# Modulation sums of a two-block transformer kernel: one-hot columns in four column groups, rows turned on VectorE

## What is computed

```python
# block one, layer l: six vectors of 1024
c_act = jax.nn.silu(c)
mod = c_act @ w_ada[l] + b_ada[l]
sh1, sc1, g1, sh2, sc2, g2 = jnp.split(mod, N_MOD, axis=-1)
h = modulate(rms_norm(x, mixer_norm_g[l]), sh1, sc1)
...
x = x + g1[:, None, :] * (mixed @ w_out[l])
h2 = modulate(rms_norm(x, ffn_norm_g[l]), sh2, sc2)
...
# block two, layer l: nine vectors of 1024
mod = (c_act @ ada_w[l] + ada_b[l])[:, None, :]
h = rmsnorm(x, norm_pre[l, 0]) * (1.0 + sc1) + sh1
y = swiglu(h, ffn_w_gate[l, 0], ffn_w_up[l, 0], ffn_w_down[l, 0])
x = x + 0.5 * g1 * rmsnorm(y, norm_post[l, 0])
```

## Time and profile before

| | |
|---|---|
| median of 3 runs (lowest to highest) | 2015.21 us (2014.39 to 2019.77) |
| profiled execution: its own time, its span | 2018.86 us, 2017.0 us |
| PE, PEld busy | 1937.6 us (96%), 1547.6 us (77%) |
| DVE, ACT, POOL busy | 1289.5 us (64%), 735.5 us (36%), 70.3 us (3%) |
| chain of waits, by engine | PE 70%, DVE 18%, issue 4%, ACT 4%, SP 2%, DMA 1%, POOL 1% |
| `ada_sum` on PE (L726) | 444 records, 52.1 us busy |
| moved by DMA | 546.99 MB, mean 271 GB/s |
| mean granted TensorE clock | 0.976 of full speed |

### The profile page before, as it was taken

How to read it: one execution, slowest core, us unless ns; L and a number is a source line. 1 busy time by engine, 2 the same in 40 slices (tenths; PEclk the granted TensorE clock), 3 DMA queues, 4 the chain that set the end, 5 groups by cost and what they waited for, 6 DMA issues and landing times.

```text
span 2017.0 us, 29866 instructions
## 1 busy us (share of the span) xinstructions
PE 1937.6 (96%) x11691; PEld 1547.6 (77%) x11691; DVE 1289.5 (64%) x2018; ACT 735.5 (36%) x1248; POOL 70.3 (3%) x111
## 2 busy tenths in 40 slices
PE   7999899998999899998999999999999999999998
PEld 7888645555888645545999887899989998878887
DVE  5999423435998324335788757666668887575555
ACT  2021222223021222224433556544464436555445
POOL 0101000000201000000000002000000000110000
PEclk6999799999999799999999999999999999999999
DMA  9859899997858799998599842677638996526651
GB/s 352 306 167 326 320 414 406 406 419 272 290 177 314 312 408 402 418 413 300 209 328 349 272 126 84 231 247 254 216 126 292 327 349 158 147 75 205 202 189 40
DMA packets 266958, 546.99 MB, mean 271 GB/s; under 512 B 31042, under 2 KB 187212, under 8 KB 242252
## 3 DMA queue, kind: packets, MB, share of 16 engines
q1 hardware_dynamic: 266828, 545.19, 74.7%
HBM read 544.08 MB, written 4.22 MB: 272 GB/s over the span
## 4 chain that ended last, share of the span: by engine, by line
PE 70%; DVE 18%; issue 4%; ACT 4%; SPq 2%; DMA 1%; POOL 1%; DVEq 0%; ACTq 0%; POOLq 0%
PE ps L859 11%; PE ps L783 10%; PE ps L709 8%; DVE acc L2083 6%; PE ps L960 6%; PE ps L740 4%; PE ps L742 4%; PE ps L741 4%; PE ps L811 3%; PE ps L770 3%; DVE arena L2217 3%; DVE wsp L2138 2%; PE ps L772 2%; PE ps L926 2%; SPq L444 2%
## 5 line engine op out<-in xcount | busy, mean ns | idle before, releaser
L2138 DVE TENSOR_TENSOR wsp<-ring,wsp 128x1024 fp32r<-128x1024 f32 x264 | 321.5, 1223 | 173.6 <-ACT wsp L1625 166.8
L1625 ACT ACTIVATE wsp<-ring 128x1024 fp32r<-128x1024 f32 x264 | 277.9, 1056 | 322.7 <-PE ps L742 196.1
L740 PE MATMUL ps<-hsp,wsp 128*128 128x256 f32 x1120 | 319.6, 285 | 5.0 <-DVE hsp L2613 3.0
L741 PE MATMUL ps<-hsp,wsp 128*128 128x256 f32 x1120 | 316.9, 283 | 0.0
L742 PE MATMUL ps<-hsp,wsp 128*128 128x256 f32 x1120 | 316.8, 283 | 0.0
L709 PE MATMUL ps<-arena,ring 128*128 128x256 f32 x1280 | 283.0, 381 | 4.1 <-PE ps L709 2.7
L709 PEld LDWEIGHTS ps<-arena,ring 128*128 128x128 f32 x1280 | 242.8, 191 | 39.0 <-issue 5.0
L783 PE MATMUL ps<-wsp,asp 128*128 128x512 f32 x1056 | 255.4, 394 | 1.6 <-DVE wsp L2138 0.2
L859 PE MATMUL ps<-ring,hpick 128*64 128x512 f32 x1024 | 230.5, 603 | 8.1 <-issue 8.1
L783 PEld LDWEIGHTS ps<-wsp,asp 128*128 128x128 f32 x1056 | 194.1, 188 | 50.1 <-DVE wsp L2138 9.7
L740 PEld LDWEIGHTS ps<-hsp,wsp 128*128 128x128 f32 x1120 | 214.8, 192 | 7.7 <-DVE wsp L2138 3.6
(11 more groups left out here) (280 smaller groups left out, 2778.3 us busy)
## 6 DMA issues: line engine op xcount, KB each, us to landing
ring<-in_w_expert_gate_dram SPq DMA_DIRECT2D x64, 1024.0 KB, 8.8
ring<-in_w_expert_up_dram SPq DMA_DIRECT2D x64, 1024.0 KB, 11.1
ring<-in_w_expert_down_dram SPq DMA_DIRECT2D x64, 1024.0 KB, 10.3
ring<-in_ada_w_dram SPq DMA_DIRECT2D x48, 1152.0 KB, 9.3
ring<-in_ffn_w_gate_dram SPq DMA_DIRECT2D x44, 1024.0 KB, 11.8
ring<-in_ffn_w_up_dram SPq DMA_DIRECT2D x44, 1024.0 KB, 13.9
ring<-in_ffn_w_down_dram SPq DMA_DIRECT2D x44, 1024.0 KB, 5.2
ring<-in_w_ada_dram SPq DMA_DIRECT2D x32, 1152.0 KB, 12.0
```

The lines of the kernel that those rows point to most:

```text
L740: mm(dst, hi, v_hi, start=start, stop=False, skip_group_check=True)
L741: mm(dst, hi, v_lo, start=False, stop=False, skip_group_check=True)
L1625: act_(split_part(at % SPLITS, 0, n), piece(unit, n), ACT.Identity).then_inc(S.whi, 1)
L2138: v_.tensor_tensor(split_part(at % SPLITS, 1, n), piece(unit, n), split_part(at % SPLITS, 0, n, F32), ALU.subtract).then_inc(S.wlo, 1)
```

## The change

- `ada_sum` gives way to `row_sum` for all units but unit 11 of block two. The stationary operand is now a window of 32 columns of `onehot` in which one column is ones and the others zeros; the moving operand is `acc`. `acc` is cut into four sets of six strips of 32 columns, and each set goes to a column group of the array of its own (PSUM partitions 0 to 31, 32 to 63, 64 to 95, 96 to 127) with 192 moving columns. So there are four matmuls of 128 x 32 by 128 x 192 where there were six of 128 x 128 by 128 x 1. The column that holds the ones chooses the row in which the unit's sums land; the other rows receive zeros, and all units of a stage add up in one bank, one row each.
- DVE adds no bias per unit. `turn_sums` transposes the bank once per stage in blocks of 32 x 32 (128 x 192) into `rowcols`, waits for it, and `add_rows` adds the bias for all units at once. The five adds of a mixer become one, and so do the eight of block two's f = 0; PE no longer waits for DVE to read a bank.
- In the opening the 32-column window of unit `u` in `chot` holds `c_act` instead of ones; blocks that PE takes from the ring go the same way. Of unit 2 PE takes blocks 4 to 7, DVE 0 to 3 (`OPENING = (6, 6, 4)`).
- `four` of f = 0 is written out twice on PE and DVE, since the window is a constant of the instruction. ACT and SP keep their loop.

```diff
-MODS = 11
+MODS = 4
+HOT, ROWS = 8, 32
+OPENING = (6, 6, 4)
...
+            def row_of(bank, v, window, start):
+
+                v = v.rearrange("p (k j n) -> p j k n", k=AC, j=P // ROWS)
+                for j in range(P // ROWS):
+                    last = mm(ps[j * ROWS:(j + 1) * ROWS, bank, 0:AC * ROWS], window, v[:, j], start=start, stop=True,
+                              skip_group_check=True)
+                return last
+
+            def row_sum(n, slot, bank, row, start):
+
+                pe.wait_ge(S.ada_acc, n + 1)
+                row_of(bank, acc[:, slot, :], hot(onehot, row), start).then_inc(S.ada_sum, 1)
...
-                def ada_later(u, bank, read):
-
-                    pe.wait_ge(S.ada_mod, read)
-                    ada_sum(u - AHEAD, (u - AHEAD) % 2, bank)
+                def ada_later(u):
+
+                    row_sum(u - AHEAD, (u - AHEAD) % 2, 4, u - AHEAD, start=(u == AHEAD))
...
                             if f == 0:
 
-                                pe.wait_ge(S.ada_mod, i * 4 + j + units_in(2) + MODS * l)
-                                ada_sum(i * 4 + j + 12 * l, j % 2, 3)
+                                row_sum(i * 4 + j + 12 * l, j % 2, 3, i * 4 + j, start=(i == 0 and j == 0))
...
-                    if f:
-                        four(0)
-                        four(1)
-                    else:
-                        with pe.Fori(0, 2) as i:
-                            four(i)
+                    four(0)
+                    four(1)
...
+            def turn_sums(ready, count, bank):
+
+                eng.wait_ge(ready, count)
+                own.link(v_.transpose(rowcols[:], ps[:, bank, 0:AC * ROWS]))
+
+            def add_rows(u, n, bias_at):
+
+                def units(v, at):
+                    return v[:, at:at + n * AC].rearrange("p (u k) -> p u k", u=n)
+                v_.tensor_tensor(units(mod, u * AC), summed(0, n), units(vA, u * AC + bias_at), ALU.add
+                                 ).then_inc(S.ada_mod, 1)
...
                 conv(1)
-                mod1(3, 5)
-                mod1(4, 4)
                 conv(2)
...
-                mod1(5, 5)
-                mod1(6, 4)
                 ada1(7)
...
+                turn_sums(S.ada_sum, 8 - AHEAD, 4)
+                add_rows(AHEAD, 8 - AHEAD, ROWS_1["ada"][0])
+                eng.wait_ge(S.ada_mod, 2)
                 ahead1(0)
-                mod1(7, 4)
                 ahead1(1)
...
-                            if f == 0:
-                                mod2(i * 4 + AHEAD + j)
...
                     if f == 0:
+                        turn_sums(S.ada_sum, 8 + 12 * l, 3)
+                        add_rows(AHEAD, 8, 0)
+                        eng.wait_ge(S.ada_mod, 2 + MODS * l)
```

More of the change, by code:

```diff
@@ L391, in release, with hot, summed @@
                 eng.sem_inc(free[unit % RING][part], 1)
-        def units_in(u):
-            return u - 1 if u >= AHEAD else 1
+        def hot(v, row):
+            return v[..., HOT - row:HOT - row + ROWS]
+        def summed(row, n=1):
+            return rowcols[:].rearrange("p (k u) -> p u k", k=AC)[:, row:row + n, :]
         def clear(eng, sems, go):
@@ L1119, in _ @@
             S = opening
-            pe.wait_ge(init_v, 1)
+            pe.wait_ge(chot_w, 1)
             for u in range(AHEAD):
[L1122 to L1127, removed]
-                last.then_inc(free[u % RING][1], 1)
[L1129 to L1134, removed]
+                for k in range(OPENING[u], KD):
+                    if k == OPENING[u] and k < 6:
+                        wait_landed(pe, 0, 0, u, parts=(0,))
+                    elif k == 6:
+                        wait_landed(pe, 0, 0, u, parts=(1,))
+                    last = row_of(6, wada(u)[:, k, :], hot(chot[:, k, :], u), start=(u == 0 and k == OPENING[0]))
+                last.then_inc(free[u % RING][1], 1)
+                row_sum(u, u % 2, 6, u, False)
             S = first
@@ L2094, in opening_unit @@
                     eng.wait_ge(S.ada_sum, u - 1)
-                for k in range(6):
+                for k in range(OPENING[u]):
                     if k == 0:
@@ L2098, in opening_unit @@
                     else:
-                        eng.wait_ge(S.ada_part, 5 * u + k)
+                        eng.wait_ge(S.ada_part, sum(OPENING[:u]) - u + k)
                         last = v_.scalar_tensor_tensor(acc[:, u % 2, :], wada(u)[:, k, :], cvec[:, k:k + 1],
                                                        acc[:, u % 2, :], ALU.mult, ALU.add)
-                    last.then_inc(S.ada_part if k < 5 else S.ada_acc, 1)
-                eng.wait_ge(S.ada_acc, u + 1)
-                release(eng, u, (0,))
+                    last.then_inc(S.ada_part if k < OPENING[u] - 1 else S.ada_acc, 1)
+                if OPENING[u] == 6:
+                    eng.wait_ge(S.ada_acc, u + 1)
+                    release(eng, u, (0,))
             def ada_mod(u, bias_at, bank, sums_before=0):
@@ L2163, in _ @@
             v_.memset(eps[:], EPS).then_inc(consts, 1)
+            own.link(v_.memset(onehot[:], 0.0))
+            v_.memset(onehot[:, HOT:HOT + 1], 1.0).then_inc(consts, 1)
+            own(v_.memset(chot, 0.0))
             eng.wait_ge(init_t, 2)
@@ L2171, in _ @@
             eng.wait_ge(init_v, 1)
+            own.wait()
+            v_.tensor_copy(chot[:, :, HOT:HOT + 1], cvec[:, 0:KD].unsqueeze(2)).then_inc(chot_w, 1)
             S = opening
@@ L2180, in _ @@
             S = first
-            n, at = AHEAD * AC, ROWS_1["ada"][0]
-            eng.wait_ge(opening.ada_sum, AHEAD)
-            v_.tensor_tensor(mod[:, 0:n], ps[:, 6, 0:n], vA[:, at:at + n], ALU.add).then_inc(S.ada_mod, 1)
+            turn_sums(opening.ada_sum, AHEAD, 6)
+            release(eng, AHEAD - 1, (0,))
+            add_rows(0, AHEAD, ROWS_1["ada"][0])
             eng.wait_ge(S.ada_mod, 1)
@@ L2685, in four @@
                             lo(18 + 6 * j, 3 + e, 2, i)
-                            if f == 0:
-                                mod2(i * 4 + AHEAD + j)
-                    if f:
-                        four(0)
-                        four(1)
-                    else:
-                        with eng.Fori(0, 2) as i:
-                            four(i)
+                    four(0)
+                    four(1)
                     if f == 0:
+                        turn_sums(S.ada_sum, 8 + 12 * l, 3)
+                        add_rows(AHEAD, 8, 0)
+                        eng.wait_ge(S.ada_mod, 2 + MODS * l)
                         eng.wait_ge(go_e, L)
```

54 lines of the change are left out of this document (26 added, 28 removed).

## The result

| | before | changed |
|---|---|---|
| median (lowest to highest) | 2015.76 us, 8 runs (2014.39 to 2020.89) | 2012.47 us, 8 runs (2005.43 to 2017.75) |
| ratio of the runs | | 0.9975, interval 0.9963 to 0.9987 |
| profiled execution: own time, span | 2018.86, 2017.0 | 2017.75, 2016.0 |
| PE, PEld busy | 1937.6, 1547.6 | 1902.9, 1488.3 |
| mean granted TensorE clock | 0.976 | 0.973 |

A second series, run later with the experiments, gave 0.9971 (0.9959 to 0.9983), with medians of 2018.38 and 2011.66. By the medians the change takes off 3.3 us in the first series and 6.7 in the second, by the ratios 5.0 and 5.9, not 13.8: it is faster, but less than forecast and outside the range of 1996 to 2009. The profiled execution is the slowest of the eight; its total says little, and the stages are read instead.

What follows compares the result with a forecast made beforehand. The prediction took DVE to bound the mixer of layer 0 and PE f = 0 of block two; 9.8 + 1.8 + 1.2 + 0.6 + 0.4 = 13.8 us off 2015.2 gave 2001.4 us, range 1996 to 2009.

Steps and rivals of the forecast that it cites:

- What bounds the kernel before: DVE bounds the mixer of layer 0 (122.8 of 135 us), PE bounds f = 0 of block two (166.2 of 167).
- The price of a sum: On PE, a sum falls from 1.26 to 0.65 us with four groups side by side, a saving of 0.61.
- Rivals 1 and 3: Sums on PE: less than four wide, 2006.6 us, chance 0.20; groups take turns, 2035 or 2020.5 us, chance 0.07.
- f = 0, 9.8 us: Block two, both layers: 16 sums at 0.61 each, with the unit falling from 18.72 to 18.11 us.
- Both loops: f = 0 of block two: one through PE's sum, 18.11 us per unit; one through the DMAs, at least 18.1.
- rival 2: f = 0 of block two: the DMA loop is tighter, half the gain (4.9) survives, 2006.3 us; chance 0.12.
- f = 1 of layer 0: Block two: three sums at 0.61 each save 1.8 us, as the unit is bound by PE.
- Mixers, 2.2 us: Both layers: 1.2 from sums in the output projection, 0.6 from adds on DVE's path, 0.4 from layer 1's channel sum.
- its cover: Mixers: DVE's 3.37 us idle at the projection's end covers the new wait; without it 0.9 per layer, 1.8 in all.
- this path: Mixers, DVE's path: adds leaving the convolution stage and unit 7's fold, four pairs, save 0.6 us.
- Opening, nothing: Opening: DVE's add moves forward some 5 us, but DVE waits for unit 3's DMA until 48.49; 0 to -0.1.
- Unrolling, nothing: Writing out `four` costs 0, since f = 1 is written out already and holds 16.98 us per unit.

Runs made afterwards that it cites:

- changed_again: The changed kernel itself, run a second time beside the experiments; 2011.66 us, 0.9971 against the kernel before.
- warm_conv: The changed kernel with 24 matmuls of unused result put ahead of the wait for the last convolution in layer 0; 2007.37 us, 0.9946.
- block_two: The kernel before with the change in block two alone, opening and both mixers as before; 2011.38 us, 0.9963.
- before_less_ada: The kernel before with only one of each three or two blocks of modulation weights loaded in f = 0 of block two; 2018.84 us, 0.9995.
- doubled version: The changed kernel with each sum of f = 0 in block two computed twice; 2007.03 us, 0.9949.

## Where the prediction was right and wrong

- **What bounds the kernel before**: right. Fewer bytes or another order of the loads gave it nothing (0.9995, 0.9993).
- **The price of a sum**: 0.65 forecast, 0.46 measured. The saving was 0.80, not 0.61. The four groups run wholly side by side: the eight records of a second sum take 0.32 us, 0.04 each, and 2 x 0.165 = 0.33 is the time of one group alone. The step that was too high is the sum of 0.15, 0.09 and 0.08 for entering, leaving and stagger, which is 0.14. Rivals 1 and 3 are refuted. The estimate from the Trainium skill's "TensorE: Matmul & The Clock Gate", Part 3 (3.2 times for four column tiles) is too low here: 8 x 0.165 = 1.32 in 0.32 is 4.1 times.
- **f = 0, 9.8 us: this step failed.** Both loops had been found, and the second put at 36.21 for two units "so a unit cannot fall below 18.1". Two of its terms were right to 0.12 us; the third, the 18.95 from the issue of the down part to ACT's piece 16, measured 19.8 to 20.4 in the two profiles of the changed kernel (once 21.1). It was read from one burst, and the trace of the kernel before had longer ones: its first three in layer 0 take 20.1, 20.0 and 19.9, the last four 18.86 to 18.95. Here is the second, from the issue to ACT's piece 16, 1036.62 - 1016.58 = 20.04:

```profile
1016.58 0.37 SPq L444 DMA_DIRECT2D ring<-in_ffn_w_down_dram  x1
...
1036.62 1.06 ACT L1625 ACTIVATE wsp<-ring 128x1024 fp32r<-128x1024 f32 x1 [3.69 <-DMA ring<-in_ffn_w_up_dram]
```

  With 20.0 in place of 18.95 the prediction's own sum gives (20.0 + 1.10 + 16.16) / 2 = 18.63 per unit, 0.1 below the pace before, so the trace at hand already spoke against 9.8 us. The unit came out at 18.45 to 18.5 (18.6 and 18.8 in layer 1, the latter with one unit of 21.2, in which the granted clock was 0.72 from 1594 to 1600 us) instead of 18.1, and the pace above 18.4 with short sums is the sign that the prediction had named for rival 2. Of 9.8 us, 0.3 and 2.9 arrived in the two profiles of the changed kernel, and 3.9 to 4.9 in the three other versions with the same code in f = 0, with the larger saving per sum unused. Rival 2 had it at half the gain, 4.9, which is the most that was seen; its total was still too low, as nothing came of block one. A bound with 0.0 us of room beside a forecast was a sign that I should have given this rival far more than 0.12, and a range that reaches beyond 2009. Why some bursts take a microsecond longer than others stays open; what was tested is that it no longer matters with gate and up first.
- **f = 1 of layer 0**: the unit with a sum went from 18.66 to 1346.42 - 1328.47 = 17.95, the one without stayed at 16.98, in the chain of the changed kernel:

```profile
1328.47 2.75 PE ps L806 x12
...
1346.42 0.69 PE ps L806 x3
...
1363.40 0.69 PE ps L806 x3
```

  0.71 per unit, three times 2.1 against the forecast 1.8, and the stage itself went from 205.4 us to 203.3. The further 0.9 in the row of the table is attention, with its place of low clock.
- **Mixers, 2.2 us: a second step that failed**, wrong in sign in layer 0 up to the second channel sum. The working counted what PE and DVE save and took the idle time that PE gains ahead of DVE for free. It was not, since the clock fell there. The note that DVE bounds this stage stood in the first paragraph; a second question, what PE does with time that it gets in a stage where it waits, was not put. The joint sum on DVE takes 1.46 us from the transposition to the next fold, against 0.9 forecast; its cover held, as DVE still waits for PE at the end of the projection, 3.48 us (3.37 before), and 1.79 in `changed_again`.

```profile
176.34 0.38 DVE L2127 STREAM_TRANSPOSE rowcols<-ps 128x192 f32<-128x192 f32 x1
176.75 1.01 DVE L2133 TENSOR_TENSOR mod<-rowcols,vec 128x30 f32<-128x30 f32 x1
177.80 0.62 DVE L2092 TENSOR_SCALAR acc<-ring,cnext 128x768 f32<-128x768 f32 x1
```

  Behind the second channel sum the mixers did gain. From its start to DVE's last add of the projection it took 206.85 - 144.59 = 62.26 us before and, in `changed_again`, 208.46 - 147.71 = 60.75:

```profile
208.46 0.88 DVE L2288 SCALAR_TENSOR_TENSOR x<-ps,mod,x 128x256 f32<-128x256 f32 x2 [1.79 <-PE ps L719]
```

  That is 1.5 less, where 0.6 was forecast for this path. The first profile of the changed kernel hides it (62.44), as its granted clock is 0.91 from 176 to 194 us and 1.00 in the two others. So in layer 0 of `changed_again` this gain paid back half of the 3.1 us that the second channel sum came late: the last add comes 1.6 us later than before, and 1.1 us earlier in `warm_conv` (205.71), where the clock held. In layer 1 the way from the end of the experts to the second channel sum went from 103.8 to 103.4 us, and from there to the end of the projection from 64.6 to 63.7, so that the two layers together come out near nothing.

- **Opening, nothing**: right in its reason. DVE's add comes at 36.69 instead of 41.88, and the fold of unit 3 waits 7.62 us for its DMA instead of 2.78, to 48.15 instead of 48.49:

```profile
36.69 0.18 DVE L2133 TENSOR_TENSOR mod<-rowcols,vec 128x18 f32<-128x18 f32 x1
...
48.15 0.62 DVE L2092 TENSOR_SCALAR acc<-ring,cvec 128x768 f32<-128x768 f32 x1 [7.62 <-DMA ring<-in_w_ada_dram]
```

- **Unrolling, nothing**: right; 17.97 per unit with the code written out.
- **What arrived, in sum**: 0.3 to 4.9 in f = 0, 2.1 in f = 1, and about nothing in block one: 2.4 to 7 us, against the 3.3 to 6.7 of the medians. So the stages account for the total, as closely as single profiles can.

## What to carry to other kernels

When an engine that bounds a stage gets faster, work out every other loop with its transfers as it will be once it is the bound, and read the time of a transfer from all of its occurrences in the trace, not from one; where both loops come out alike, as here, count on losing part of the gain, and look at the queue that issues them: a load whose buffer has long been free may stand behind one whose buffer is not. Order the issues of a queue by when their buffers come free and when they are needed. And in a stage that another engine bounds, time taken off TensorE is not neutral: it becomes idle time at a wait, and can cost the clock of the work behind it.

## What the runs showed of the hardware

- Four column groups overlap without loss: 0.32 us for eight records of 192 columns in four groups, where 1.32 would be due one after another. Entering and leaving them cost 0.14 us together.
- The same work of PE behind a wait took 0.70 us after 0.61, 0.91, 1.04 and 2.08 us of idle time (`warm_conv`, before, `block_two`, `before_less_ada`), and 1.22 after 3.51 and 5.74, with the granted clock at half. In the doubled version it took 1.22 in layer 1 too, after 2.78 us. Kernels whose code differs only in block two spread by 5 us in block one. Over the nine runs of the changed kernel in the second series the time goes from 2008.8 to 2016.7 us as the mean granted clock goes from 0.982 to 0.975, and the kernel before from 2014.1 to 2020.7 us between 0.979 and 0.975: at one and the same clock the changed kernel is some 2 to 5 us faster.
- A mean DMA share of 0.93 in f = 0 was no ceiling: with the loads issued in three lots the engines ran at 0.96 and 327 GB/s in layer 0, and all waits for them were gone.
